# Inverses of a chunked recurrence on 32x32 blocks, their products in four pieces, and low-rank products on both row halves

## The reference

```python
def step(state, inp):
    r_t, w_t, k_t, v_t, a_t, b_t = inp
    sa = jnp.einsum('bhvk,bhk->bhv', state, a_t)
    state = (state * w_t[:, :, None, :]
             + sa[..., :, None] * b_t[:, :, None, :]
             + v_t[..., :, None] * k_t[:, :, None, :])
    y = jnp.einsum('bhvk,bhk->bhv', state, r_t)
    return state, y
```

```python
decay_log = -jax.nn.softplus(-(w0 + jnp.tanh(w_lo) @ w_decay_up)) - 0.5
a = jax.nn.sigmoid(a0 + a_lo @ w_aaa_up)
```

## Time and profile before

| | us |
|---|---|
| median of three runs | 4276.49 |
| profiled execution | 4283.65 |
| its span | 4281.8 |
| PE busy | 3858.1 |
| DVE busy | 1958.1 |
| ACT busy | 1442.7 |
| POOL busy | 989.7 |

### The profile page before, as it was taken

The page is one execution under the profiler, slowest core; times in us unless marked ns, Lnnn a source line. Parts: engine busy times, 40 slices in busy tenths (PEclk is TensorE's granted clock), DMA queues, the critical chain, the costliest instruction groups (busy, mean ns, idle before and its releaser), DMA issues.

```text
span 4281.8 us, 67153 instructions
## 1 busy us (share of the span) xinstructions
PE 3858.1 (90%) x29532; PEld 2367.6 (55%) x29532; DVE 1958.1 (46%) x2105; ACT 1442.7 (34%) x1807; POOL 989.7 (23%) x438
## 2 busy tenths in 40 slices
PE   6989999999999999998899888989788988988887
PEld 3556666666666665456544455555554455555454
DVE  3456455654554653441323255254552255254552
ACT  4222223233222312231213233454453233454452
POOL 2413323342332322031252200111002200111102
PEclk9999999999999999999999988999999988999999
DMA  2111111111111113232311200100012100100002
GB/s 97 56 36 46 39 43 56 41 51 46 53 49 41 60 46 145 96 138 99 138 64 51 80 10 11 40 23 23 25 51 84 36 10 11 36 24 20 30 24 90
DMA packets 61586, 226.95 MB, mean 53 GB/s; under 512 B 6832, under 2 KB 8560, under 8 KB 60784
## 3 DMA queue, kind: packets, MB, share of 16 engines
q1 hardware_dynamic: 52224, 189.64, 12.9%
q10 hardware_dynamic: 9072, 33.03, 1.9%
HBM read 174.93 MB, written 47.71 MB: 52 GB/s over the span
## 4 chain that ended last, share of the span: by engine, by line
PE 73%; DVE 17%; ACT 6%; DMA 2%; issue 2%; POOL 1%; DVEq 0%; SPq 0%; ACTq 0%; POOLq 0%
PE psum L1000 71%; DVE arena L2110 7%; DVE arena L2113 5%; ACT arena L1572 4%; PE psum L1003 2%; DVE arena L2502 2%; DVE arena L2568 2%; ACT wh L1572 1%; DMA arena<-in_w_proj_conv 1%; POOL hl L2627 1%; POOL arena L2627 0%; DVE arena L2117 0%; DMA arena<-in_w_in 0%; POOL wl L2627 0%; ACT arena L2044 0%
## 5 line engine op out<-in xcount | busy, mean ns | idle before, releaser
L1000 PE MATMUL psum<-arena 64*64 64x32 f32 (+12 forms) x18860 | 1452.3, 276 | 250.7 <-DVE arena L2110 89.2
L1000 PEld LDWEIGHTS psum<-arena 64*64 64x64 f32 (+6 forms) x18860 | 1045.1, 157 | 686.8 <-issue 378.6
L2627 POOL TENSOR_TENSOR wl<-arena,wh 128x1024 bf16<-128x1024 f32 (+1 forms) x203 | 493.2, 2430 | 2248.5 <-ACT wh L1572 2245.4
L1000 PE MATMUL psum<-hh,wh 128*128 128x512 f32 x3248 | 913.0, 423 | 73.3 <-ACT hh L1572 24.3
L1000 PE MATMUL psum<-hh,wl 128*128 128x512 bf16 x3248 | 825.3, 394 | 1.6 <-POOL wl L2627 1.6
L1572 ACT ACTIVATE arena<-psum 128x512 f32<-128x512 f32 (+4 forms) x660 | 415.8, 630 | 1156.7 <-PE psum L1000 856.3
L1000 PE MATMUL psum<-hl,wh 128*128 128x512 bf16 x3248 | 773.2, 384 | 8.0 <-POOL hl L2627 8.0
L1000 PEld LDWEIGHTS psum<-hh,wh 128*128 128x128 f32 x3248 | 609.5, 194 | 276.0 <-issue 50.8
L2110 DVE TENSOR_TENSOR arena<-psum,arena 128x512 f32<-128x512 f32 (+3 forms) x488 | 319.4, 654 | 894.5 <-PE psum L1000 596.6
L2113 DVE SCALAR_TENSOR_TENSOR arena<-arena 128x1024 f32<-128x1024 f32 x356 | 571.4, 1605 | 165.1 <-ACT arena L1572 148.7
L2627 POOL TENSOR_TENSOR arena<-arena 128x1024 f32<-128x1024 f32 (+4 forms) x142 | 362.2, 2550 | 869.4 <-ACT arena L1572 460.4
(11 more groups left out here) (37 smaller groups left out, 805.9 us busy)
## 6 DMA issues: line engine op xcount, KB each, us to landing
arena<-in_w_in SPq DMA_DIRECT2D x161, 512.0 KB, 3.5
scr_g<-arena ACTq DMA_DIRECT2D x24, 512.0 KB, 2.7
arena<-scr_g SPq DMA_DIRECT2D x24, 512.0 KB, 4.5
arena<-in_w_out SPq DMA_DIRECT2D x24, 512.0 KB, 3.5
arena<-in_w_mem_kv SPq DMA_DIRECT2D x16, 512.0 KB, 3.5
scr_x<-arena SPq DMA_DIRECT2D x16, 512.0 KB, 3.6
arena<-scr_x SPq DMA_DIRECT2D x16, 512.0 KB, 6.8
arena<-in_x SPq DMA_DIRECT2D x8, 512.0 KB, 10.8
```

What stands on the lines that cost most here:

```text
L1000: return pe.e.matmul(o, l, r, start=start, stop=stop)
L2627: return pool.seq.tensor_tensor(o, a, b, op)
```

## The change

The inverse stops at blocks of 32. The two 32x32 blocks on the diagonal of each 64x64 matrix are kept apart: X, XT and Y have 32 columns a chunk instead of 64 (`XD`, `XTD`, `YD`), and the four row quarters of the partitions hold the four blocks of the two heads. The products of levels 0 to 4 are 64 matmuls each of 32 rows, 32 columns of weights and 16 moving columns, on the four diagonal quarters of the array. Their results fill half a bank. Level 5 has the two products of the off-diagonal quarter alone (`lower_left`, 32 matmuls each). ACT and DVE copy its first result into `YL`; ACT and POOL spread `XTD` into the whole XT (`whole`), and ACT and DVE add the last quarter to it.

Each product is given out in four pieces (`inverse`), with a yield between. The projections in this stage come in parts of 3 matmuls instead of 12, for a quarter of a step. `lora` is split by positions instead of by matrix: its two matmuls take rows 0 to 63 and rows 64 to 127, and ACT applies its sigmoids in halves of 512 columns.

A block's `late` has 21 steps before and 29.75 after (3 x 0.25 + 0.5 for a product, for `sp` 4 x 0.25). Counted from the list, blocks 1 to 4 take 606 matmuls of projections each (492 before), and from block 7's first step to `merge(0)` there are 96 (864 before). The pieces of a block's 15 products stand in 60 groups between other work in blocks 0 to 6 (11 before), and in 5 in block 7 (11 before).

The diff, cut to its core:

```diff
     def shifted(what, ct, col):
-        yield from P((what, ct), A["w_in"][col], "h", deep=4)
+        yield from P((what, ct), A["w_in"][col], "h", deep=1, share=0.25)
         do("shift", what, ct)
...
-        for i in range(2):
-            two(("lora", ct, i), ("lora", ct, i))
-            do("lsig", ct, i)
+        for c in range(2):
+            two(("lora", ct, c), ("lora", ct, c))
+            do("lsig", ct, c)
...
+    def inverse(name, ct, lv):
+
+
+        ps.take((name, ct, lv), 1, SM)
+        ps.keep((name, ct, lv), 1)
+        for j in range(4):
+            if j:
+                yield 0.25
+            do(name, ct, lv, j)
+
...
-            one(("sx", ct, lv), ("sx", ct, lv), SM)
+            yield from inverse("sx", ct, lv)
             do("sxe", ct, lv)
+            ps.leave(("sx", ct, lv))
             if lv == 0:
                 for g in range(2):
                     one(("ta", ct, g), ("ta", ct, g), SM)
             if lv in (2, 3):
                 for g in range(2 * lv - 4, 2 * lv - 2):
                     one(("bt", ct, g), ("bt", ct, g), SM)
-            yield
+            yield 0.5
             if lv == 0:
                 continue
             if lv < 5:
-                one(("sp", ct, lv), ("sp", ct, lv), SM)
-            one(("sq", ct, lv), ("sq", ct, lv), SM)
+                yield from inverse("sp", ct, lv)
+                yield 0.25
+            yield from inverse("sq", ct, lv)
             do("sqe", ct, lv)
-            yield
+            for name in ("sp", "sq") if lv < 5 else ("sq",):
+                ps.leave((name, ct, lv))
+            if lv == 4:
+                do("whole", ct)
+            yield 0.5
         do("decay", ct)
         for name, n in (("w0", 2), ("tu", 4), ("mr", 4)):
...
-            yield from P(("glu_b", ct), A["w_in"][41 + ct], "h", deep=4)
+            yield from P(("glu_b", ct), A["w_in"][41 + ct], "h", deep=1, share=0.25)
...
-        for _ in late(ct) if ct < NT else range(21):
-            states.step()
-            other.step(1.0 if ahead.live else 1.4)
-            ahead.step()
+        for part in late(ct) if ct < NT else [1] * 21:
+            part = part or 1
+            states.step(part)
+            other.step(part * (1.0 if ahead.live else 1.4))
+            ahead.step(part)
             if live["taps"]:
-                live["taps"].step(1.5)
+                live["taps"].step(1.5 * part)
...
-        def lora(ct, i):
-            use = ("lora", ct, i)
+        def lora(ct, c):
+
+            use = ("lora", ct, c)
             cleared(use)
             pe.wait_ge(*at(f"lora_in{ct % 2}", ct))
             pe.wait_ge(*at("lo"))
-            r = slice(64 * i, 64 * i + 64)
-            for c in (0, 512):
-                x = mm(pair(use)[:, c:c + 512], LW[ct % 2][r, :], lo[r, c:c + 512])
-            x.then_inc(*pe.up("lora", ct, i))
+            for i in range(2):
+                r = slice(64 * i, 64 * i + 64)
+                x = mm(pair(use)[:, 512 * i:512 * i + 512], LW[ct % 2][r, :], lo[r, 512 * c:512 * c + 512])
+            x.then_inc(*pe.up("lora", ct, c))
 
...
-        def solve(name, ct, lv, l, r):
+        def solve(name, ct, lv, j, l, r):
 
             o, m = bank((name, ct, lv)), 1 << lv
-            for n in range(NCH):
+            for n in range(4 * j, 4 * j + 4):
+                for q in range(4):
+                    p = slice(32 * q, 32 * q + 32)
+                    x = mm(o[p, 16 * n:16 * n + 16].rearrange("p (b m) -> p b m", m=m), l(p, n, q), r(p, n))
+            if j == 3:
+                x.then_inc(*pe.up(name, ct, lv))
+
+        def lower_left(name, ct, to, j, l, r):
+
+            o = bank((name, ct, 5))
+            for n in range(4 * j, 4 * j + 4):
                 for h in range(2):
-                    p = slice(64 * h, 64 * h + 64)
-                    x = mm(o[p, 32 * n:32 * n + 32].rearrange("p (b m) -> p b m", m=m), l(p, n, h), r(p, n))
-            x.then_inc(*pe.up(name, ct, lv))
-
-        def sx(ct, lv):
-            cleared(("sx", ct, lv))
+                    p, q = (slice(64 * h + a, 64 * h + a + 32) for a in (32 - to, to))
+                    x = mm(o[q, 32 * n:32 * n + 32], l(p, n, h), r(p, n))
+            if j == 3:
+                x.then_inc(*pe.up(name, ct, 5))
+
+        def sx(ct, lv, j):
+            if j == 0:
+                cleared(("sx", ct, lv))
             pe.wait_ge(*at("Gm", ct, 3, 1))
             pe.wait_ge(*(at("X", ct, lv - 1) if lv else at("eye", ct)))
-            solve("sx", ct, lv, lambda p, n, h: G[p, n, h, 0:64], lambda p, n: half(ch(X)[p, n], 0, 1 << lv))
-
-        def sp(ct, lv):
-            cleared(("sp", ct, lv))
+            if lv == 5:
+                lower_left("sx", ct, 32, j, lambda p, n, h: G[p, n, h, 32:64], lambda p, n: ch(XD)[p, n])
+            else:
+                solve("sx", ct, lv, j, lambda p, n, q: G[p, n, q // 2, 32 * (q % 2):32 * (q % 2) + 32],
+                      lambda p, n: half(ch(XD)[p, n], 0, 1 << lv))
+
+        def sp(ct, lv, j):
+            if j == 0:
+                cleared(("sp", ct, lv))
             pe.wait_ge(*at("Ym", ct, lv))
             pe.wait_ge(*(at("XT", ct, lv - 1) if lv > 1 else at("XT0", ct)))
-            solve("sp", ct, lv, lambda p, n, h: ch(XT)[p, n], lambda p, n: half(ch(Y)[p, n], 0, 1 << lv))
-
...
+            pe.wait_ge(*at("whole_l", ct))
+            pe.wait_ge(*at("whole_q", ct, 0))
+            pe.wait_ge(*at("whole_q", ct, 1))
...
+        def sxe(ct, lv):
+            if lv == 5:
+                act.wait_ge(*at("sx", ct, 5))
+                f(YL[32:64], cols3(bank(("sx", ct, 5)), NCH)[32:64], AF.Copy).then_inc(*act.up("YL", ct, 0))
+
+        def whole(ct):
+            act.wait_ge(*at("XT", ct, 4))
+            if ct:
+                act.wait_ge(*at("tu", ct - 1, 3))
+            f(ch(XT)[:, :, 0:32], ch(XTD), AF.Copy, scale=upper).then_inc(*act.up("whole_l", ct))
+
+        def sqe(ct, lv):
+            if lv == 5:
+                act.wait_ge(*at("sq", ct, 5))
+                act.wait_ge(*at("whole_r", ct))
+                f(ch(XT)[0:32, :, 32:64], cols3(bank(("sq", ct, 5)), NCH)[0:32], AF.Copy).then_inc(*act.up("whole_q", ct, 0))
...
+                cp(ch(XT)[64:96, :, 32:64], cols3(bank(use), NCH)[64:96]).then_inc(*dve.up("whole_q", ct, 1))
...
+            pool.seq.memset(YD, 0.0).then_inc(*pool.up("Yz", ct, lv))
+
+        def whole(ct):
+            pool.wait_ge(*at("XT", ct, 4))
+            if ct:
+                pool.wait_ge(*at("tu", ct - 1, 3))
+            pool.seq.tensor_copy(ch(XT)[:, :, 32:64], ch(XTD)).then_inc(*pool.up("whole_r", ct))
```

More of the change, by code:

```diff
@@ L220, in build @@
     id64 = cst[:, C_ID64:C_ID64 + 64]
-    ymt = cst[:, C_YT:C_YT + 32]
-    ymask = [cst[:, C_YM + 64 * i:C_YM + 64 * i + 64] for i in range(6)]
+    id32 = cst[:, C_ID32:C_ID32 + 32]
+    upper = cst[:, C_UP:C_UP + 1]
+    ymt = cst[:, C_YT:C_YT + 16]
+    ymask = [cst[:, C_YM + 32 * i:C_YM + 32 * i + 32] for i in range(5)]
     rst = cst[:, C_RST:C_RST + 1024]
@@ L474, in chain @@
             yield
-        yield from P(("gate", ct), A["w_in"][25 + ct], "h", deep=4)
+        yield from P(("gate", ct), A["w_in"][25 + ct], "h", deep=1, share=0.25)
         do("gout", ct)
@@ L495, in side @@
             do("glu_s", ct)
-            yield from P(("glu_a", ct), A["w_in"][33 + ct], "h", deep=4)
+            yield from P(("glu_a", ct), A["w_in"][33 + ct], "h", deep=1, share=0.25)
             if live["taps"]:
@@ L502, in side @@
             for kind, col, c_ in todo[5 * ct:5 * ct + 5] if ct < 7 else todo[35:]:
-                yield from P((kind, c_), A["w_in"][col + c_], "h", deep=4)
+                yield from P((kind, c_), A["w_in"][col + c_], "h", deep=1, share=0.25)
                 side_s.take((kind, c_))
@@ L1672, in kn, with lsig @@
             f(bt1, bt1, AF.Exp, bias=L12, scale=-0.5).then_inc(*act.up("kinv", ct))
-        def lsig(ct, i):
+        def lsig(ct, c):
             table(SIGMOID)
-            act.wait_ge(*at("lora", ct, i))
-            if ct and i:
+            act.wait_ge(*at("lora", ct, c))
+            if ct and c == 0:
                 act.wait_ge(*at("bk_pool", ct - 1))
                 act.wait_ge(*at("bk_dve", ct - 1))
-            elif ct:
                 act.wait_ge(*at("ar0", ct - 1))
-            f((bsg, ba_)[i], pair(("lora", ct, i)), AF.Sigmoid, bias=V(("w0", "a0")[i], ct)).then_inc(*act.up("lsig", ct, i))
-            ps.give(("lora", ct, i), ("lsig", ct, i))
+            s, p = slice(512 * c, 512 * c + 512), pair(("lora", ct, c))
+            f(bsg[:, s], p[:, 0:512], AF.Sigmoid, bias=V("w0", ct)).then_inc(*act.up("lsig_w", ct, c))
+            f(ba_[:, s], p[:, 512:1024], AF.Sigmoid, bias=V("a0", ct)).then_inc(*act.up("lsig_a", ct, c))
+            ps.give(("lora", ct, c), ("lsig_a", ct, c))
         def cs(ct):
@@ L2691, in sxe @@
                 return
-            x_ = half(XT, 1, 1).rearrange("p (n b) m -> p n (b m)", n=NCH)
```

(22 more changed lines are left out.)

77 lines of the change are left out of this document (48 added, 29 removed).

## The result

The changed kernel takes 4495.84 us (median of four runs, 4487.36 to 4502.66) against 4277.07 in the same session: a ratio of 1.0511 with a 95% interval of 1.0489 to 1.0533, 219 us more. The forecast was 4256, with 4225 to 4338 as its range: the sign was wrong, and the time lies 158 us above the upper end.

What follows compares the result with a forecast made beforehand. PE was taken as the bound (90% busy), so time is its work plus its waits. Terms -12 - 7 - 7 + 4 = -22 on the median 4276.49 gave 4254.5, stated as 4256 us, range 4225 to 4338.

Steps and rivals of the forecast that it cites:

- Term 1: Low-rank products (`lora`), two in each of 8 blocks: two pairs of records instead of four single ones, -12 us.
- Term 2: Levels' products on PE, blocks 0 to 6: pieces of 0.495 us, entries and exits taking nearly all the saving, -7 us.
- D: Rival for the levels' products: a group of four quadrant records needs 56 ns whatever the width, 4341 us; chance 0.17.
- E: Rival: quadrants don't run side by side, one record per 0.030 us stays, 4276 + 290 us; chance 0.05.
- Term 3: End of the stage, block 7 to merge 0: moved projections neither gain nor lose, block 7's products need no entries, -7 us.
- rival C: End without filler: block 7's chain, handovers and state steps bare, PE at slow clock, 4308 us (4268 to 4315); chance 0.28.
- Term 4: PE's waits in the levels: shorter DVE reads against thinner projection cover, +4 us, bounds -12 and +35.
- groups of four, pieces and `lora`: Signs: 8 groups in some 0.25 us, a piece with entry 0.5 us, `lora` in pairs, 1.7 us a block less.
- block to block: Sign: distance between blocks up from about 190 us to about 212 in blocks 1 to 5.
- the end more than 125: Sign: last block's G to merge 0 down from 281 to about 102 us; over 125, C holds.
- waits before levels: Sign: waits before the levels' records 16 us or less.

Runs made afterwards that it cites:

- e1: The kernel before with only the low-rank products (`lora`) split by positions, two row halves at once: 4258.81 us, ratio 0.9961.
- e8: e2 with the two products of a couple half a step apart and projections still in parts of 12: 4263.76 us, ratio 0.9959 to the kernel before.
- e10: The changed kernel with each product in two pieces, projections in parts of 12, streams half a step out of phase: 4262.80 us, ratio 0.9967 to the kernel before.
- e2: The changed kernel with each product given out whole, the old yields and projections in parts of 12: 4296.14 us, ratio 1.0042 to the kernel before.

## Why the prediction was wrong, point by point

- **Term 1** (-12) was right: -18 in e1, with an interval that reaches to -11, and -14 by its own rows (16 times 0.85); the rest went with less slow clock.
- **Term 2** (-7) was right. A piece takes 0.37 us from its first start to the next matmul and 0.09 to 0.11 for its entry, 0.46 to 0.49 against 0.495 (pieces alone between projections, full clock). What it had too low is a state step beside a piece, 0.26 us instead of 0.12. Terms 1 and 2 together were to bring -17 us in blocks 0 to 6; what is left there behind waits and clock is between -7 and +7. D and E are refuted: a group of four takes 34 ns, near the 30 taken, not 56 or 120.
- **Term 3** (-7) failed: the end took 138.9 instead of 102 us, so +30. This is rival C, whose term 3 was +31, for its clock (0.71 over the stretch) and its bare handovers (24.4 us idle), and for one thing that no rival had: instructions at 256 in 3.3 us (8.9 of the 24.4 us are under "issue"). But C's whole time, 4268 to 4315, is far from what came.
- **Term 4** (+4, bounds -12 and +35) is the step that broke the forecast. It counted the levels' waits, and even they went from 10.7 to 31.8 us in blocks 0 to 6, most of it in one wait a block behind a `shift` on DVE. And the sentence of term 3, "Nothing is gained or lost by the 768 moved ones", took the projections for filler that never waits. But a projection needs its PSUM pair back, and that distance had also fallen, from 12 matmuls to 0 or 3. It stood in the same order of the list from which I had read the cover of the levels, and I counted there only the products. This was 91 us of waits, and the slow clock behind all waits 61 to 75, for which the sum had nothing in the blocks. No rival had either: all but E end at 4341 or below, and E, which ends higher, is refuted.
- Of what was to show it: groups of four, pieces and `lora` came out right; block to block took 239 to 250 us in blocks 1 to 5 instead of 212, the end more than 125, and waits before levels more than 16.

The largest version of the gain that was found is e1, e8 or e10, all 0.3 to 0.4% faster than before and not told apart from each other. The quadrants' saving of some 75 us in blocks 0 to 6 (e2 against e1: +54 waits, +52 for the clock, yet only +30 in all) has not reached the total in any of them.

## What to carry to other kernels

When filler is cut finer, count for every buffer that it rotates, not only for the work it hides, how much stands between its last use and its next; a list of the order tells this before any run. Count the slow clock behind waits as well: here 114 us more of waits came with 166 us more at 1.2 GHz, an estimated 61 to 75 us. Before idle time is read as waiting, compare the counts of weight loads and matmuls. And when instructions become small, compare their rate with the code's: here it was 13 ns each.

## What the runs showed of the hardware that was not expected

PE's instructions come in blocks of 256, started never closer than 3.3 us, and a burst of 512 in 2.2 us stops PE for some 2 us in its second half. Records of 32x16 on four quadrants in turn start 7 ns apart at the median. In blocks 0 to 6 of the changed kernel 23 of the 24 waits of 2.5 us and more, and 13 of the 15 waits of 2 to 2.5 us, ended in a stretch at 1.2 GHz or within 1.5 us of its start; the stretches lasted 3.4 to 17.1 us.
